# Two transformer blocks on one core: the last small embedding product behind the last gate, the last squares summed in TensorE, three normalized tiles on Pool

## The reference, cut to what matters

```python
h3 = rmsnorm_2(x, ln3[i])
x = x + jax.nn.sigmoid(h3 @ w_pg[i]) * (p[i] @ w_pp[i])
return rmsnorm_2(x, ln_f)     # x * rsqrt(mean(x*x) + EPS) * ln_f
```

## Time and profile before

| what | us |
|---|---|
| median of 3 runs | 1979.49 (1978.73 to 1979.78) |
| the profiled execution's own time | 1977.24 |
| its span | 1975.4 |
| TensorE matmul busy | 1927.7 (98%) |
| VectorE busy | 958.7 (49%) |
| ScalarE busy | 775.4 (39%) |
| Pool busy | 60.1 (3%) |

### The profile page before, as it was taken

The page is one execution under the profiler, slowest core; times in us unless marked ns, Lnnn a source line. Parts: engine busy times, 40 slices in busy tenths (PEclk is TensorE's granted clock), DMA queues, the critical chain, the costliest instruction groups (busy, mean ns, idle before and its releaser), DMA issues.

```text
span 1975.4 us, 30845 instructions
## 1 busy us (share of the span) xinstructions
PE 1927.7 (98%) x12860; PEld 1599.1 (81%) x12860; DVE 958.7 (49%) x1515; ACT 775.4 (39%) x1212; POOL 60.1 (3%) x117
## 2 busy tenths in 40 slices
PE   7999988999999999999999999999999999999996
PEld 5887788868788888888699978888888888888885
DVE  6548634455454344347643236544344544344436
ACT  5364543372353234245442252323422442133343
POOL 0000000000140000000001100000000000000000
PEclk9999999999999999999999999999999999999998
DMA  4222100014432222222322222222233322222222
GB/s 169 96 77 84 65 24 5 7 64 135 136 120 96 96 96 96 96 96 86 117 75 86 86 85 97 86 75 75 91 112 118 107 96 96 96 97 97 97 84 85
DMA packets 52448, 177.91 MB, mean 90 GB/s; under 512 B 7871, under 2 KB 8399, under 8 KB 52320
## 3 DMA queue, kind: packets, MB, share of 16 engines
q1 hardware_dynamic: 45184, 161.50, 24.4%
q0 software_dynamic: 6448, 13.41, 2.2%
q10 hardware_dynamic: 688, 1.11, 0.2%
HBM read 169.67 MB, written 5.47 MB: 89 GB/s over the span
## 4 chain that ended last, share of the span: by engine, by line
PE 94%; DVE 3%; ACT 1%; DMA 1%; issue 1%; ACTq 0%; DVEq 0%; SPq 0%
PE bank L663 93%; DMA ring<-in_stream 1%; DVE ring_lo L1847 1%; PE bank L845 0%; PE bank L727 0%; DMA x<-in_xT 0%; ACT ring_hi L1339 0%; DVE work_r L1903 0%; ACT work L1339 0%; PE bank L1269 0%; DVE nr L1861 0%; PE bank L817 0%; DVE hf L1883 0%; DVE work_r L1852 0%; DVE bias L2075 0%
## 5 line engine op out<-in xcount | busy, mean ns | idle before, releaser
L663 PE MATMUL bank<-work_r,ring_hi 128*128 128x512 f32 x2592 | 810.3, 391 | 14.5 <-DVE ring_lo L1847 13.2
L1847 DVE TENSOR_TENSOR ring_lo<-ring,ring_hi 128x1024 fp32r<-128x1024 f32 x302 | 367.8, 1224 | 617.4 <-ACT ring_hi L1339 617.3
L663 PEld LDWEIGHTS bank<-work_r,ring_hi 128*128 128x128 f32 x2592 | 488.0, 188 | 119.2 <-DVE ring_lo L1847 13.8
L1339 ACT ACTIVATE ring_hi<-ring 128x1024 fp32r<-128x1024 f32 x302 | 318.4, 1057 | 541.8 <-DMA ring<-in_stream 539.4
L663 PE MATMUL bank<-work_r,ring_lo 128*128 128x512 f32 x1296 | 506.4, 391 | 0.0
L663 PE MATMUL bank<-h_hi,ring_hi 128*128 128x512 f32 x864 | 340.1, 394 | 1.0 <-DVE ring_lo L1847 1.0
L663 PE MATMUL bank<-h_hi,ring_lo 128*128 128x512 f32 x864 | 336.4, 389 | 0.0
L663 PEld LDWEIGHTS bank<-work_r,ring_lo 128*128 128x128 f32 x1296 | 244.5, 189 | 50.7 <-issue 0.7
L663 PE MATMUL bank<-h_lo,ring_hi 128*128 128x512 f32 x864 | 212.2, 389 | 0.0
L663 PEld LDWEIGHTS bank<-h_hi,ring_hi 128*128 128x128 f32 x864 | 162.2, 188 | 41.3 <-issue 6.9
L663 PEld LDWEIGHTS bank<-h_hi,ring_lo 128*128 128x128 f32 x864 | 162.2, 188 | 34.4 <-issue 1.2
(11 more groups left out here) (227 smaller groups left out, 1571.8 us busy)
## 6 DMA issues: line engine op xcount, KB each, us to landing
ring<-in_stream SPq DMA_DIRECT2D x302, 512.0 KB, 3.3
x<-in_xT POOLq DMA_DIRECT2D x8, 256.0 KB, 3.0
spill<-x POOLq DMA_DIRECT2D x1, 2048.0 KB, 11.3
work<-x POOLq DMA_DIRECT2D x32, 64.0 KB, 2.0
x<-spill POOLq DMA_DIRECT2D x8, 256.0 KB, 2.9
outT<-hf SPq DMA_DIRECT2D x8, 256.0 KB, 2.1
x<-in_xT ACTq DMA_DIRECT2D x2, 512.0 KB, 8.4
x<-in_xT SPq DMA_DIRECT2D x2, 512.0 KB, 6.9
```

The lines of the kernel that those rows point to most:

```text
L663: ins = pe.matmul(out, lhsT, rhs, start=start, stop=stop, skip_group_check=True)
L1339: return nc.scalar.activation(out, in_, func, **kw)
L1847: v.tensor_tensor(ring_lo[:, n % RING, :, :], ring[:, n % RING, :, :], ring_hi[:, n % RING, :, :], ALU.subtract).then_inc(sem("split_lo"), 1)
```

## The change

- The last small product of the second block, ("pp", 2, 7), goes from ahead of the eight gates to behind the last of them. Its weights get a block of their own at the end of the stream (`last`, the 303rd). ScalarE no longer copies it; VectorE multiplies straight from its bank with the gate.
- In the second block, VectorE scales gate m behind product and add of tile m - 1, not ahead of them. The square sum of tile 6 stands ahead of product and add of tile 7.
- The squares of tile 7 aren't added by VectorE: `last_squares` multiplies the sum of the first seven and then the squares of tile 7 by ones, into one bank.
- ScalarE writes x * ln_f of tiles 0, 1 and 2 to W(0..2) while the gates run (`gained`); at the end Pool multiplies these by the root (`y_pooled`), and VectorE makes only tiles 3 to 7. SyncE stores in the order 3, 4, 0, 5, 6, 1, 7, 2.

```diff
@@ block_counts
-            ("ff1_2", 16), ... ("ple2", 2), ("gate2", 8)]
+            ("ff1_2", 16), ... ("ple2", 2), ("gate2", 8), ("last", 1)]
@@ tail_jobs
-    j += [("pp", blk, m) for m in range(PLE_BEFORE_SUM, DT)]
-    j += [("pg", blk, m) for m in range(DT)]
-    return j if blk == 1 else j + [("ss", first + 2)]
+    j += [("pp", blk, m) for m in range(PLE_BEFORE_SUM, DT - 1)]
+    gates = [("pg", blk, m) for m in range(DT)]
+    return j + [("pp", blk, DT - 1)] + gates if blk == 1 else j + gates + [("pp", blk, DT - 1), ("ss", first + 2)]
@@ SyncE
-            for m in range(DT):
-                sp.wait_ge(sem("y_out"), m + 1)
+            for m in (3, 4, 0, 5, 6, 1, 7, 2):
+                if m in POOLED:
+                    sp.wait_ge(sem("y_pooled"), m + 1)
+                else:
+                    sp.wait_ge(sem("y_out"), m - len(POOLED) + 1)
@@ Pool
+            for i in POOLED:
+                pool.wait_ge(sem("gained"), i + 1)
+                pool.wait_ge(sem("root"), 7)
+                pool.tensor_tensor(hf[:, i, :], W(i), nr[:, 0, :], ALU.mult).then_inc(sem("y_pooled"), 1)
@@ TensorE
+            def last_squares(n):
+                out = take("ss", n)
+                pe.wait_ge(sem("sq_added"), added(n) + DT - 2)
+                pe.matmul(out[:, :], ONES, nr[:, 1, :], start=True, stop=False, skip_group_check=True)
+                pe.wait_ge(sem("sq"), DT * n + DT)
+                pe.matmul(out[:, :], ONES, W(TMP + (DT - 1) % 4), start=False, stop=True,
+                          skip_group_check=True).then_inc(bank_full[nth("ss", n)], 1)
@@ TensorE, tail
                 if blk == 2:
-                    squares(n0 + 2)
+                    project(("pp", 2, DT - 1), pieces, 2 * ((DT - 1) % 4), 2)
+                    done_with(1)
+                    last_squares(n0 + 2)
@@ ScalarE, tail
-                for m in range(DT):
+                for m in range(DT if blk == 1 else DT - 1):
                     split_hi(blocks_to("pp", blk, m))
@@
                         square(n0 + 2, m - 1)
+                        if blk == 2 and m - 1 in POOLED:
+                            f(W(m - 1), x[:, m - 1, :], ACT.Copy, scale=V("ln_f_2", m - 1)).then_inc(sem("gained"), 1)
@@ VectorE, tail (last_add and gate_scaled hold the steps of before; for tile 7 last_add reads the bank of "pp" 7)
                 for m in range(DT + 1):
-                    if m < DT:
-                        ...
+                    if blk == 1 and m < DT:
+                        gate_scaled(m)
+                    if m == DT and blk == 2:
+                        add_square(n0 + 2, m - 2)
                     if m:
-                        ...
+                        last_add(m - 1)
...
-                    elif m > 1:
+                    elif 1 < m < DT:
                         add_square(n0 + 2, m - 2)
+                    if blk == 2 and m < DT:
+                        gate_scaled(m)
...
-                else:
-                    add_square(n0 + 2, DT - 1)
@@ VectorE, end
-            normed(7, "ln_f_2", lambda i: hf[:, i, :], "y_out", nr[:, 0, :])
+            for i in range(len(POOLED), DT):
+                v.scalar_tensor_tensor(out=hf[:, i, :], in0=x[:, i, :], scalar=V("ln_f_2", i), in1=nr[:, 0, :],
+                                       op0=ALU.mult, op1=ALU.mult).then_inc(sem("y_out"), 1)
```

More of the change, by code:

```diff
@@ L64 @@
 PLE_BEFORE_SUM = 5
+POOLED = range(3)
 NORM_EPS = 1e-6
@@ L103, in block_counts @@
             ("hk", 4), ("hq", 4), ("hv", 8), ("att_v", 12), ("hr", 8), ("att_qk", 24), ("gates2", 8), ("merge2", 20), ("out2", 8),
-            ("ff1_2", 16), ("ff2_2", 16), ("ff1b_2", 16), ("ff2b_2", 16), ("ple2", 2), ("gate2", 8)]
+            ("ff1_2", 16), ("ff2_2", 16), ("ff1b_2", 16), ("ff2b_2", 16), ("ple2", 2), ("gate2", 8), ("last", 1)]
 def block_starts():
@@ L299, in weight_block @@
         return BS["att_v"] + 4 * VALUE_GROUPS.index(at[0]) + 2 * at[1]
+    if job == ("pp", 2, DT - 1):
+        return BS["last"]
     if name in ("wo", "f1", "f2", "pp", "pg"):
@@ L1138, in tail @@
                 pe.wait_ge(sem("p_lo"), 2 * blk)
-                for m in range(DT):
-                    project(("pp", blk, m), plain(lambda k: R(37 + k), lambda k: R((39, 44)[k])), 2 * (m % 4), 2)
-                    if m % 4 == 3:
+                pieces = plain(lambda k: R(37 + k), lambda k: R((39, 44)[k]))
+                early = DT if blk == 1 else DT - 1
+                for m in range(early):
+                    project(("pp", blk, m), pieces, 2 * (m % 4), 2)
+                    if m % 4 == 3 or m == early - 1:
                         done_with(1)
@@ L2285, in tail, with last_add, gate_scaled @@
                 scale_of(n0 + 1)
+                def last_add(m):
+                    dve.wait_ge(sem(f"ple_gate{blk}"), m + 1)
+                    if blk == 2 and m == DT - 1:
+                        dve.wait_ge(*computed("pp", blk, m))
+                        v.tensor_tensor(W(m), bank(("pp", blk, m))[:, :], W(8 + m % 4),
+                                        ALU.mult).then_inc(bank_drained[nth("pp", blk, m)], 1)
+                        dve.wait_ge(*is_drained("pp", blk, m))
+                    else:
+                        dve.wait_ge(*is_drained("pp", blk, m))
+                        v.tensor_tensor(W(m), W(m), W(8 + m % 4), ALU.mult).then_inc(dve_step, tick())
+                        dve.wait_ge(dve_step, count["step"])
+                    v.tensor_tensor(xt(m), xt(m), W(m), ALU.add).then_inc(sem(f"x3_{blk}"), 1)
+                def gate_scaled(m):
+                    split_lo(blocks_to("pg", blk, m if m > TOGETHER else 0))
+                    dve.wait_ge(*computed("pg", blk, m))
+                    v.tensor_tensor(W(8 + m % 4), bank(("pg", blk, m))[:, :], nr[:, 0, :], ALU.mult).then_inc(bank_drained[nth("pg", blk, m)], 1)
                 for m in range(DT + 1):
-                    if m < DT:
-                        split_lo(blocks_to("pg", blk, m if m > TOGETHER else 0))
-                        dve.wait_ge(*computed("pg", blk, m))
-                        v.tensor_tensor(W(8 + m % 4), bank(("pg", blk, m))[:, :], nr[:, 0, :], ALU.mult).then_inc(bank_drained[nth("pg", blk, m)], 1)
+                    if blk == 1 and m < DT:
+                        gate_scaled(m)
+                    if m == DT and blk == 2:
+                        add_square(n0 + 2, m - 2)
                     if m:
[L2292 to L2296, removed]
+                        last_add(m - 1)
                     if m == TOGETHER - 1 or m == TOGETHER:
@@ L2612, in weight_stream @@
     parts += halves(a["w_mlp1_2"][0], a["w_mlp2_2"][0])
-    parts += [four(a["w_pp_2"][0]), column_blocks(a["w_pg_2"][0])]
+    parts += [four(a["w_pp_2"][0]), column_blocks(a["w_pg_2"][0]), four(a["w_pp_2"][0])[1:2]]
     return np.concatenate(parts, 0)
```

1 line of the change is left out of this document (removed).

## The result

The changed kernel takes 1983.93 us (median of 8 runs, 1982.23 to 1986.44), the kernel before 1978.78 (median of 8 runs beside them, 1976.21 to 1979.78): a ratio of 1.0028, 95% interval 1.0019 to 1.0038. It is slower, by 5.2 us, where 2.5 faster had been forecast, and it lies outside the range. The profiled execution took 1983.79, its span 1981.9.

A forecast was written before the change was run, and what follows sets the result against it. TensorE was taken to bound the kernel until the last gate product, then three engines by turns. Gains of 0.76 + 1.70 + 0 = 2.46 us gave 1974.8 for the profiled execution, 1977.0 for the median; range 1976.2 to 1980.2.

The forecast's parts named there:

- What bounds the kernel: Whole span: TensorE, 94% of it, until the last gate product ends; then single instructions of three engines by turns.
- the tail in three parts: Behind the last gate, 18.2 us: 5.52 to the squares' product, 4.74 through the Exp, 7.98 for tiles and stores.
- Part 1: Small product moved behind the gates: 1.36 us leave TensorE's stream, less a stall of 0.60, so 0.76 gained.
- The upper bound of 0.7: TensorE's stall in the first gates: 0.7 us if the weight load of 0.19 comes in full on top.
- The cover of the new block: Moved product's own weight block: ready near 1947, ten us before the product, so cost 0.
- Part 2: Behind the last gate: VectorE's new order and the last squares on TensorE start the Ln 1.70 us earlier.
- G: End of the last gate product, 1957.16 us in the kernel before; the tail of 18.2 us starts there.
- The wait for the square of tile 6: VectorE behind the last gate: waits about 1.1 us for ScalarE's square, giving back the shorter chain; reordering worth 0.05.
- Part 3: Tiles and stores at the end: three tiles on Pool and a new store order gain nothing, 0 to 0.1 us.
- rival A: Tiles at the end: VectorE and Pool exclude each other over SBUF reads, 2.4 to 2.8 us lost; chance 33%.
- N: Start of the normalized tiles at the end; from it to the end of the span, 7.98 us before the change.
- Rival B: Tiles at the end: Pool slow, costing from 1.8 us a tile on, kernel slower above 2.6; chance 8%.

The follow-up runs named there:

- the squares alone: Kernel before with only VectorE's new order and the last squares on TensorE; small product and all eight tiles as before: 1978.66 us, one run.
- Pool's tiles alone: Kernel before with only ScalarE's three gained tiles, Pool's three products and the new store order: 1984.91 us (median of 5), ratio 1.0037.
- Pool first: Changed kernel, but VectorE waits until Pool has made its three tiles before making its own: 1979.15 us, one run.

## Why the prediction was wrong

**What bounds the kernel, and the tail in three parts.** Right: the first two stages came as they were counted.

**Part 1.** Forecast 0.76 (0.65 to 0.9); 0.63 in the changed kernel, and 0.60 to 0.91 in the seven others that have it. The stop is where it was put and has the releaser that was named. With the slower matmuls right behind it, it was sized at 0.60 and costs 0.73 in the changed kernel, 0.45 to 0.76 over all eight. What moves it is the DMA of that block: where it took 3.23, TensorE stopped for 0.30; where it took 3.47, as in the changed kernel, for 0.53; where it took 3.55, for 0.61. The upper bound of 0.7 doesn't follow from its own terms either: 0.60 and the whole weight load of 0.19 are 0.79. The cover of the new block holds: no kernel shows a wait of TensorE for it.

**Part 2.** Forecast Ln at G + 5.90, last square at G + 3.96, full clock; measured 5.92, 3.98, full clock (1.10 and 1.12 for the two ones products). The wait for the square of tile 6, forecast at about 1.1, is 1.22, and taking it away gave back 1.1. That the moved product is what keeps the clock was argued from its place in the tail; the squares alone show it, with 0.6 lost. VectorE was forecast idle for 1.4 before the last gate's end and is for 1.35. The forecast 1.70 measured 1.68.

**Part 3.** Forecast 0, measured 6.8, and two steps failed.

The first is "from there the stores need 0.69 each, whoever makes the tiles". It took VectorE's 0.66 and Pool's 1.23 as if side by side. Pool's own price was right (1.25), the sum of the two was not: beside a Pool tile a VectorE tile takes 1.75 and Pool's 1.71, one of each in 1.67, less than the 0.66 + 1.22 = 1.88 of the two apart. This was rival A, with 33%, and its mechanism came: it said that the span would end at N + 10.4 to 10.8, and the stores with 0.4 behind them would have ended it at N + 11.2 in the changed kernel, where one store landed late, and at N + 10.3 with Pool's tiles alone. The Trainium skill (SBUF — State Buffer, Who interferes with whom) says that a VectorE instruction with two SBUF inputs and a GpSimd instruction that reads SBUF block each other, and the runs agree: each Pool tile costs VectorE 1.0, and memsets cost it nothing. For the whole length, as the prediction put it, is more than they show: 1.0 of a Pool tile of 1.25, and 1.67 for a pair instead of 1.88. By that rule A should have had the larger chance, since the prediction had no row against it, only none for it. The prediction's estimate of 1.1 to 1.2 for Pool's tile, from the Trainium skill (GPSIMD Engine Reference, Performance versus the Vector engine), is near the 1.25 that Pool takes when VectorE is silent.

The second is the sentence "Pool has nothing queued behind these three". Behind them stands the drain, and no step, no bound and no rival had it. Rival B asked how long Pool's tiles may take and let Pool's part end with its last store; but from Pool's last instruction it is 9.3 + 0.3 to the end of the program. An estimate from the table: the span of before ends at N + 8.0, so Pool may work until N - 1.6 (8.0 less 9.6) for nothing, and each us later costs one, as 1.5, 1.9, 3.8, 5.2 and 5.6 do there. With the tiles starting at N, no duration of Pool's tiles could have made part 3 free; even at VectorE's 0.66 a tile they would have ended near N + 2 and the span near N + 11.7. The row was in the trace of before, with its 9.292, one line of the program that every engine ends with; it was hidden there and wasn't asked for.

The two costs don't add. The stores are 3.2 later in the changed kernel (7.6 to 10.8), of which about 0.9 is likely the one late landing, since Pool's tiles alone, with the same times for the tiles, have 2.3; the span ends 3.6 behind where those stores would have ended it, and 6.8 is what is seen. Exclusion has a share in the 6.8 through Pool's own lateness: with Pool first the drain, and the span, end 1.4 earlier.

The sum: 2.31 gained (0.63 + 1.68) and 6.8 lost is 4.5 slower; the medians say 5.2, with an interval of 3.8 to 7.5. The range ended at the price of A and had 6% for slower, all of it in B.

## What to carry to other kernels

Before work is given to an engine near the end of a program, read what that engine's queue still holds behind it, the drain at the program's end too: an instruction that costs nothing because it lies early has its price when it is moved late, and on Pool that was 9.3 us from its last work, or from a wait behind it, in every kernel here. Two engines share a job only if their operands let them: with two SBUF inputs on VectorE and reads on Pool, eight tiles went from 5.4 to 6.4 us through Pool's help.

## What the runs showed of the hardware

- Pool's drain lasts 9.29 us when a wait comes last (from 1558.6 in the kernel before, 3.4 behind Pool's last instruction), and otherwise until 9.3 us behind its last instruction: 9.42 for a memset of 0.1, 14.2 for three tiles. The drains of VectorE and ScalarE end with or right behind their engines' last work. Why Pool's takes so long no run here shows.
- VectorE's 128x512 product of two SBUF tiles takes 1.75 instead of 0.75 when a Pool tile of 1.25 runs beside it, and isn't touched by Pool's memsets of 0.52 for a tile of the same size.
- The view of waits laid SyncE's 3.9 at the end to TensorE's queue. It was Pool's drain, found only among the instructions of the end of the block.
- TensorE's granted clock fell from 2.4 to 1.2 GHz in the midst of the last ones product when there was no product between the last gate and the sums (idle 2.8, then 1.10 of work, then idle 0.80), and didn't fall before the Ln when six matmuls stood in that gap. With the six matmuls and then nothing until G + 5.52 it fell 5.7 behind G, with nothing at all 4.5 behind G.
- The stop in the first gates follows the landing of one weight block of 512 KB: 0.30 for a DMA of 3.23, 0.61 for one of 3.55.
